# Expert stage with eight experts known beforehand, five of them loaded when it begins, and down weights issued by ScalarE

## The reference, cut to what matters

```python
N_GROUPS, EXP_PER_GROUP, TOP_K, D_EXPERT = 4, 8, 2, 256       # 32 experts
h2 = modulate(rmsnorm(x, g_ffn), sh_m, sc_m)
x = x + gt_m[:, None, :] * hier_moe(h2, ...)

def hier_moe(h, ...):
    g_logits = h @ w_rg + b_rg;  g_sel = argmax(g_logits)      # one group of eight
    e_logits = h @ w_re + b_re                                 # inside it, the best two experts
    top_v, top_i = lax.top_k(e_in, TOP_K)
    w2 = softmax(top_v) * p_g
    a = h @ w_gate[e];  b = h @ w_up[e]                        # 1024 x 256 each
    act = silu(a) * b * gate
    return act @ w_down[e]                                     # 256 x 1024
```

## Time and profile before

| | |
|---|---|
| timed runs | 1287.98, 1291.29, 1291.51 us; median 1291.29 |
| profiled execution, its own time | 1291.53 us |
| its span | 1289.9 us (19011 instructions) |
| PE busy | 1182.8 us (92%), ACT 356.3 (28%), DVE 672.3 (52%), POOL 212.8 (16%) |
| expert stage's first list read to the end | 968.8 to 1289.9 us |
| DMA over the span | 213.47 MB, mean 165 GB/s |
| weight loads of 1024 KB by SP in the expert stage | 84 |

### The profile page before, as it was taken

How to read it: one execution, slowest core, us unless ns; L and a number is a source line. 1 busy time by engine, 2 the same in 40 slices (tenths; PEclk the granted TensorE clock), 3 DMA queues, 4 the chain that set the end, 5 groups by cost and what they waited for, 6 DMA issues and landing times. The chain is left out here.

```text
span 1289.9 us, 19011 instructions
## 1 busy us (share of the span) xinstructions
PE 1182.8 (92%) x7174; PEld 662.3 (51%) x7175; DVE 672.3 (52%) x1313; ACT 356.3 (28%) x781; POOL 212.8 (16%) x250
## 2 busy tenths in 40 slices
PE   4999999999978997899999999899976999977995
PEld 1555555555543556666677776555543433332331
DVE  1255443554465884567777775544462554433443
ACT  1122222222222444265555553323320000000000
POOL 4000000000000002254443322011022212211111
PEclk9899999999998998889999999899977999988998
DMA  8721211111137871421111005362447999999993
GB/s 361 297 66 33 66 53 46 53 45 54 41 122 226 300 275 58 124 58 30 29 29 30 2 1 165 121 231 89 184 152 285 337 367 367 382 395 377 357 348 65
DMA packets 92834, 213.47 MB, mean 165 GB/s; under 512 B 20673, under 2 KB 54707, under 8 KB 77394
## 3 DMA queue, kind: packets, MB, share of 16 engines
q1 hardware_dynamic: 82258, 195.02, 41.1%
q0 software_dynamic: 7200, 17.33, 5.4%
q10 hardware_dynamic: 3296, 0.02, 0.1%
HBM read 185.03 MB, written 34.13 MB: 170 GB/s over the span
## 5 line engine op out<-in xcount | busy, mean ns | idle before, releaser
L2404 PE MATMUL g_GU<-w_gu,first_region 128*32 128x512 f32 (+2 forms) x656 | 143.0, 624 | 17.0 <-issue 17.0
L1921 PE MATMUL f_C<-first_region,oT 128*128 128x512 f32 x256 | 115.2, 603 | 0.0
L454 PE MATMUL U<-region,b_hT 128*128 128x512 f32 x256 | 112.3, 592 | 0.0
L2614 DVE TENSOR_TENSOR g_sig<-g_GU,g_sig 128x256 f32<-128x256 f32 x23 | 9.8, 425 | 165.8 <-ACT g_sig L2564 157.7
L1723 DVE TENSOR_TENSOR_SCAN region<-region,early 128x128 f32<-128x128 f32 (+7 forms) x64 | 88.6, 1404 | 6.3 <-POOL region L1530 6.3
L2404 PEld LDWEIGHTS g_GU<-w_gu,first_region 128*32 128x32 f32 (+2 forms) x656 | 43.2, 127 | 84.3 <-issue 83.4
L454 PE MATMUL b_UL<-region,b_hT 128*128 128x384 f32 (+1 forms) x256 | 76.5, 458 | 3.3 <-DMA region<-w_in 3.3
L1921 PEld LDWEIGHTS f_C<-first_region,oT 128*128 128x128 f32 x256 | 48.0, 193 | 54.3 <-issue 54.2
L454 PEld LDWEIGHTS U<-region,b_hT 128*128 128x128 f32 x256 | 47.5, 190 | 54.2 <-issue 54.0
L2383 POOL DMA_INDIRECT y<-oT,g_li x23 | 36.4, 1584 | 227.0 <-DVE oT L2632 133.8
L1592 PE MATMUL e_Z<-first_region,region 104*128 104x512 f32 (+3 forms) x192 | 70.8, 507 | 0.1
(11 more groups left out here) (489 smaller groups left out, 2160.2 us busy)
## 6 DMA issues: line engine op xcount, KB each, us to landing
w_gu<-w_gate SPq DMA_DIRECT2D x21, 1024.0 KB
w_gu<-w_up SPq DMA_DIRECT2D x21, 1024.0 KB
w_down<-w_down SPq DMA_DIRECT2D x21, 1024.0 KB
region<-w_ada SPq DMA_DIRECT2D x16, 1024.0 KB, 7.0
region<-w_in SPq DMA_DIRECT2D x3, 2048.0 KB, 17.5
oT<-w_gate SPq DMA_DIRECT2D x6, 1024.0 KB
oT<-w_up SPq DMA_DIRECT2D x6, 1024.0 KB
oT<-w_down SPq DMA_DIRECT2D x6, 1024.0 KB, 20.2
```

The costliest lines, as they stand in the source:

```text
L454: end = nc.tensor.matmul(dst[0:T, 0:c1 - c0], lhsT=hT[:, k, 0:T], rhs=g.w_in[:, k, c0:c1], start=k == 0, stop=k == KD - 1)
L1921: end = nc.tensor.matmul(C[n % 2][:, c * 512:(c + 1) * 512], lhsT=g.oT[:, i, k, :], rhs=wo[:, k, c * 512:(c + 1) * 512], start=k == 0, sto ...
L2404: end = nc.tensor.matmul(GU[h * n:h * n + n, :], lhsT=xT[:, b, k, h * n:h * n + n], rhs=wgu[s][:, :, k, :], start=k == 0, stop=k == KD - 1 ...
L2614: mark(nc.vector.tensor_tensor(sig[:], GU[:, 0:DE], sig[:], ALU.mult))
```

## The change

Eight experts are fixed in place of four: 0, 8, 16, 24, 4, 12, 20 and 28 in positions 0 to 7. Five of them are loaded in the norm stage in place of four. The fifth lies in a new region, slot_region, that holds the norm stage's modulation rows (f_rows in the old code) until the last tile is done. The fourth slot's loads are issued ahead of the last store of h2, right behind the last store of x2; the fifth slot's loads stand where the fourth's stood.

The fixed experts don't have a whole block each any more. They go four in three blocks (96 and 32 rows), so blocks 0 to 5 hold all eight. There are still 23 blocks: 18 of the form 96 and 32, three pairs and two whole ones (before: 12, five and six).

In the expert stage SP issues gate and up only, and waits for gu_mm only. The down weights are issued by ACT on its own queue, after the copy of the hidden values of block b for the experts whose slot was last used by block b-1. The lists of blocks 0 and 1 are read by two DMAs each.

The diff, cut to its core:

```diff
-FIXED = 4
+EVERY = 4
+FIXED, RESIDENT = NE // EVERY, 5
@@ phase_fr
-        rows = m.sb("f_rows", [P, 3, 2, D])
+        rows = g.slot_region[:].rearrange("p (a b n) -> p a b n", a=3, b=2)
@@ phase_fr, sync: the loop over tiles
+                if n == END:
+                    sp.wait_ge(pr_mm, NT)
+                    load_gate_up(nc, io, g, sp, early[3], 3, g.wgu_in[3])
+                    load_down(nc, io, g, sp, early[3], 3, g.wd_in[3])
                 sp.wait_ge(h2_done, n + 1)
                 sp.dma_start(g.h2_dram[i * P:i * P + T, :], h2[0:T]).then_inc(st_h2, 16)
                 if n in (1, 2, 6):
                     q = min(n - 1, 2)
-                    load_gate_up(nc, io, g, sp, q * EPG, q, g.wgu_in[q])
-                    load_down(nc, io, g, sp, q * EPG, q, g.wd_in[q])
-            sp.wait_ge(pr_mm, NT)
-            load_gate_up(nc, io, g, sp, 3 * EPG, 3, g.wgu_in[3])
-            load_down(nc, io, g, sp, 3 * EPG, 3, g.wd_in[3])
+                    load_gate_up(nc, io, g, sp, early[q], q, g.wgu_in[q])
+                    load_down(nc, io, g, sp, early[q], q, g.wd_in[q])
+            load_gate_up(nc, io, g, sp, early[4], 4, g.wgu_in[4])
+            load_down(nc, io, g, sp, early[4], 4, g.wd_in[4])
...
-                row = b * EPG * REGION
-                sp.dma_start(g.li[b][:], g.list_dram[row:row + P, :]).then_inc(g.li_in[b], 16)
+                list_parts(nc, g, sp, b, blocks[b], fixed_expert)
@@ phase_fr, vector: four more small steps at the start, one at the end
+            for half in range(EPG // EVERY):
+                sortable = groups(key[:])[:, :, half * EVERY + 1:(half + 1) * EVERY]
...
@@ expert_blocks
-    fixed = [whole(p) for p in range(FIXED)]
-    blocks = fixed[0:3] + paired[0:1] + fixed[3:4] + fours[0] + fours[1] + paired[1:2] + single[0:1] + paired[2:3]
-    return blocks + single[1:2] + paired[3:4] + fours[2] + fours[3] + paired[4:5]
+    fixed = [four_in_three([p, p + 1, p + 2], p + 3) for p in range(0, FIXED, NG)]
+    blocks = fixed[0] + fixed[1] + paired[0:1] + single + fours[0] + fours[1] + paired[1:2] + fours[2] + fours[3]
+    return blocks + paired[2:3]
@@ phase_g, sync: weights
                 load_gate_up(nc, io, g, sp, expert(p), s, wgu_in[s])
-                if instead[p] is not None:
-                    sp.wait_ge(dn_mm, instead[p] + 1)
-                load_down(nc, io, g, sp, expert(p), s, wd_in[s])
-            for p in order[FIXED:]:
+            for p in order[RESIDENT:]:
                 weights(p)
@@ phase_g, scalar
+            late = order[RESIDENT:]
+            def down_in(p):
+                load_down(nc, io, g, act, expert(p), place[p], wd_in[place[p]])
+            for p in late:
+                if instead[p] is None:
+                    down_in(p)
...
                 if b + AHEAD < NB:
                     list_in(b + AHEAD)
+                for p in late:
+                    if b and instead[p] == b - 1:
+                        act.wait_ge(dn_mm, b)
+                        down_in(p)
```

More of the change, by code:

```diff
@@ L1758, in phase_fr @@
         ORDER = [0, PT] + list(range(1, PT))
+        blocks = expert_blocks()
+        early = []
+        for parts in blocks:
+            early += [fixed_expert(p) for p, _, _, _ in parts if p < FIXED and fixed_expert(p) not in early]
         GW = 8
@@ L2129, in constants @@
                 step(V.tensor_copy(cum[0:1, 0, :], first_row[0:1, :]))
-                step(V.tensor_scalar(ei[:], pair[0:NE, 0, 0, 0:1].bitcast(I32), EPG - 1, None, ALU.bitwise_and))
+                step(V.tensor_scalar(ei[:], pair[0:NE, 0, 0, 0:1].bitcast(I32), EVERY, None, ALU.bitwise_and))
+                step(V.tensor_scalar(own[:], ei[:], 0.0, None, ALU.is_gt))
+                step(V.tensor_scalar(ei[:], pair[0:NE, 0, 0, 0:1].bitcast(I32), EVERY - 1, None, ALU.bitwise_and))
                 step(V.tensor_scalar(rank[:], ei[:], 0.0, None, ALU.is_equal))
@@ L2133, in constants @@
                 step(V.tensor_scalar(base[:], pair[0:NE, 0, 0, 0:1], 1.0 / EPG, -float(FIXED), ALU.mult, ALU.add))
+                step(V.scalar_tensor_tensor(base[:], own[:], NG - EVERY / EPG, base[:], ALU.mult, ALU.add))
                 step(V.tensor_scalar(base[:], base[:], rank[:], float(FIXED), ALU.mult, ALU.add))
@@ L2251, in _ @@
             step(V.scalar_tensor_tensor(key[:], count[:], float(NE), idx[:], ALU.mult, ALU.add))
-            sortable = groups(key[:])[:, :, 1:]
-            step(V.scalar_tensor_tensor(sortable, grank[:].unsqueeze(2).broadcast_to([P, NG, EPG - 1]), -SIDE / 2.0, sortable,
-                                        ALU.mult, ALU.add))
+            for half in range(EPG // EVERY):
+                sortable = groups(key[:])[:, :, half * EVERY + 1:(half + 1) * EVERY]
+                step(V.scalar_tensor_tensor(sortable, grank[:].unsqueeze(2).broadcast_to([P, NG, EVERY - 1]), -SIDE / 2.0,
+                                            sortable, ALU.mult, ALU.add))
             step(V.tensor_tensor(eq[0:NE], key[0:NE], g.ident[0:NE, 0:NE], ALU.mult))
@@ L2257, in _ @@
             others = eq[0:NE, 0:NE - FIXED]
-            step(V.tensor_scalar(others.rearrange("p (a e) -> p a e", a=NG), groups(key[0:NE])[:, :, 1:], own[:], None,
+            step(V.tensor_scalar(others.rearrange("p (a e) -> p a e", a=FIXED), lots(key[0:NE])[:, :, 1:], own[:], None,
                                  ALU.is_gt))
@@ L2284, in load_down, with fixed_expert, list_parts @@
     engine.dma_start(g.w_down[b][:], io["w_down"][e].rearrange("(p k) n -> p k n", p=P)).then_inc(sem, 16)
+def fixed_expert(p):
+    return p % NG * EPG + p // NG * EVERY
+def list_parts(nc, g, engine, b, parts, expert):
+    for p, row, n, at in parts:
+        engine.dma_start(g.li[b][at:at + n, :], g.list_dram[bass.ds(expert(p) * REGION + row, n), :]).then_inc(g.li_in[b], 16)
 def expert_blocks():
@@ L2332, in phase_g @@
         holding = {}
-        order = list(range(FIXED)) + [p for p in order if p >= FIXED]
         for q, p in enumerate(order):
@@ L2433, in _ @@
         def _(sp):
-            experts = {r: r * EPG for r in range(FIXED)}
+            experts = {p: fixed_expert(p) for p in range(FIXED)}
             def expert(r):
@@ L2789, in program @@
             g.w_down.append(part[:, 2 * KD * DE:2 * KD * DE + 2 * D].rearrange("p (k n) -> p k n", n=D))
+        g.slot_region = m.sb("slot_region", [P, 2 * KD * DE + 2 * D])
+        g.w_gu.append(g.slot_region[:, 0:2 * KD * DE].rearrange("p (w k n) -> p w k n", w=2, k=KD))
+        g.w_down.append(g.slot_region[:, 2 * KD * DE:].rearrange("p (k n) -> p k n", n=D))
         g.y = turned[:, 6 * KD * P:8 * KD * P].rearrange("p (b n) -> p b n", b=2)
@@ L2794, in program @@
         phase_fr(nc, io, g)
-        for b in range(FIXED, 6):
-            weight_slot(b)
+        weight_slot(5)
         phase_g(nc, io, g)
```

2 lines of the change are left out of this document (added).

## The result

| | us, median | span of the runs | ratio to before, 95% interval |
|---|---|---|---|
| before | 1291.4 | 1287.98 to 1291.95 (6 runs) | 1 |
| after | 1297.61 | 1296.29 to 1299.15 (6 runs) | 1.0053 [1.0043, 1.0063] |

The changed kernel is slower by some 6 us. That lies inside the predicted range (1282 to 1301), but 5 us above the predicted value, and beyond the 0.3% that I had called no change. "Slower" had a chance of 0.29 from me, "no change" 0.40. The profiled execution took 1296.73 us with a span of 1295.1; before, the span was 1289.9.

What follows compares the result with a forecast made beforehand. The expert stage was taken as bound by PE, with late weights costing 24.0 us. Terms: 1291.5 + 0 - 1.9 + 1.3 + 1.8 + 0.7 - 0.7 = 1292.7, against the median 1292.5; range 1282 to 1301 us.

Steps and rivals of the forecast that it cites:

- A fifth expert loaded ahead: Expert stage: three loads (7.7 us) leave it, but the lead is lost to full slots; taken as 0, bounds -3.1 to 0.
- The ledger's first stall: Expert stage: count of loads and per-block work put PE's first wait at block 12 or 13, 3 to 8 us.
- The later stalls: Expert stage from block 13 on: both kernels need the same experts at the same blocks, so these waits were left unchanged.
- SP doesn't wait for dn_mm: SP's queue in the expert stage: DMA idle time at 1190 us goes; -1.9 us, bounds -4.7 to 0.
- Down loads on ACT's queue: Expert stage: downs under way can hold up urgent gate and up loads; +1.3 us, bounds 0 to 10.2.
- End of the norm stage: SP's queue before the expert stage: more loads ahead of the list reads delay its start; +1.8 us, bounds +0.4 to +5.3.
- Blocks 1 and 2, and the gather of block 2: Early expert stage: longer blocks cost +0.7 us, a gather landing sooner gives -0.7; the two cancel.
- The second queue takes its turns: Rival, expert stage: each of four stalls grows by a whole down load, 10.2 us, giving 1301.6 us; chance 0.12.
- POOL's results out: Rival, expert stage: result transfers become the bound, deciding from about 12.1 us per landing; +11.9, 1305.2 us; chance 0.08.
- The lead holds: Rival, expert stage: the fifth expert's lead and all saved idle time reach PE, giving about 1283 us; chance 0.28.
- the DMA share from 980 to 990: Sign, early expert stage: this share of the DMA engines' time falls well under 0.9.
- the idle time of g_GU: Sign, PE in the expert stage: the prediction is wrong if this falls under 10 us or rises over 25.

Runs made afterwards that it cites:

- e3: Changed kernel with four experts loaded ahead in place of five, norm-stage loads at their old places: 1297.32 us, ratio 1.0067.
- e1: Changed kernel with the down loads back on SP's queue in the old order, behind its wait for dn_mm: 1291.35 us, ratio 1.0018.
- e2: Kernel before with only the down loads moved to ACT's queue: 1297.22 us, ratio 1.0060.
- e8: Changed kernel with ACT issuing each down one turn before its expert's first use, not when its slot is free: 1292.34 us, ratio 1.0013.
- e11: Kernel before with each down on SP's queue behind gate and up loads of experts that start no later: 1290.55 us, ratio 0.9997.
- e4: Changed kernel with all expert-stage loads on SP's queue in the order of need: 1291.85 us, ratio 1.0014.
- e6: Changed kernel with lists read into partitions in another order, spreading their empty places: 1301.95 us, ratio 1.0102.
- e5: Kernel before with lists read into partitions in another order, spreading their empty places: 1300.51 us, ratio 1.0076.

## Why the prediction was half right

- **A fifth expert loaded ahead: 0.** The stage is as long with four as with five (290.1 and 289.9 us from block 0 to 22), as the value says; e3's level median leaves a doubt of 3 us. On one queue the lead was gone early: by 1040 us e1 had moved 28.6 loads and the kernel before 29.4 (the bytes of SP's and ACT's queues from 971 us on, and three loads for each expert loaded ahead). Of this, 1.0 load is e1's later start, 2.6 us.
- **The ledger's first stall, at block 12 or 13, 3 to 8 us.** Wrong for the changed kernel, where none came until block 16; right for e1 (5.32 us at block 12). The later stalls, which I had let stand, went at block 15 and rose at 16 and 19, from 5.17 and 1.46 us to 10.87 and 10.71. The ledger counted every load in one line. With the downs on a queue of their own, block 12's gate and up loads had no waiting down ahead of them.
- **SP doesn't wait for dn_mm: -1.9 (-4.7 to 0).** Too small. The early share rose from e1's 0.81 to 0.95, worth up to 6.3 us by 1040. A part of that only makes good the idle time of e1's full slots: against the kernel before (0.93) the changed kernel was 1.9 loads ahead by 1040 (31.3 against 29.4), 4.9 us. I had looked for the gap of the earlier trace rows at 1190 and taken the early idle time for full slots alone.
- **Down loads on ACT's queue: +1.3 (0 to +10.2).** This is the step that failed, in its size. Together with the gain just named I had -0.6 us for the split; it cost 4.5 us net in the new order (after against e1, by the ratios) and 7.7 in the old one (e2 against before). I had argued that a down can only disturb a gate and up load while both are under way, and that ACT issues none while PE stands still. What counts is the whole stage: the downs that had run ahead by the time of a stall, 1.7 and 3.0 loads, each 2.56 us. With 1.33 downs per block (1.4 MB in 11.76 us) on a queue of its own, ACT's queue is seldom behind, while SP's is; that could have been worked out beforehand.
- **End of the norm stage: +1.8 (+0.4 to +5.3).** 3.2 in the profile, and 2.9 between e3's wait for the list and this one; inside the bounds.
- **Blocks 1 and 2, and the gather of block 2.** Right. X's wait of 0.73 us for that gather went, and 0.94 came for the hidden values in its place.
- **The rivals.** *The second queue takes its turns* named the mechanism nearly: late gate and up loads, at the price of whole downs. It had four stalls grow by one down each. They became two, 5.7 and 9.3 us longer than before, with 1.7 and 3.0 downs ahead of them. The Trainium skill (DMA: Bandwidth & Descriptors, Queues, rings and completion order) says that each DMA engine goes round robin between the queues that have work. The rows agree in part: q1 and q10 had 49.9% and 25.3% of the engines' time up to block 19, not equal halves, as q10 has only half as many bytes to bring. Here the queue with little to bring kept up (25.0 downs, all that could be issued), and the one that was late got the rest. *POOL's results out*: they landed after 12.6 us as I had worked out (12.7), which is over the 12.1 from which I had them decide, but PE waited for them 1.08 us. The stalls for weights hid the rest. e8, with results nearly as slow, has the time back. *The lead holds* was true from block 13 to 15, 11.5 us ahead, and false at the end.
- **The range.** It held the time partly by luck: an early gain that I had too small and an overtaking that I had much too small stand against each other. Of the signs, the DMA share from 980 to 990 fell as foretold (0.71, 1.00 before), and the idle time of g_GU stayed between 10 and 25 us (21.6), but no stall came at block 12 or 13.
- The Trainium skill (the same page, Issuing engines are not separate DMA queues) says that issuing from several engines saves only the sequencer's time. These runs disagree in both directions: 0.81 to 0.95 of DMA share early, as a wait on one queue no longer holds the other, and 4.5 us lost in all, because the order of service changed.

In the changed kernel the granted clock was 0.62 over the stall at block 16, which is the 1.2 GHz level for most of it, and 0.72 over the 9.70 us of products behind it (stretches as above):

```profile
1170.80:1181.70 10.90, 0.04 (x1) 0.02 (x1) 2.83 (x3) 0.39 (x1) 0.45 (x1) 0.62 1.02 374
1181.70:1191.40 9.70, 9.69 (x66) 2.69 (x66) 1.22 (x2) 0.00 (x0) 2.17 (x2) 0.72 0.96 348
1196.30:1203.30 7.00, 7.00 (x69) 2.19 (x72) 1.29 (x2) 0.39 (x1) 1.36 (x2) 1.00 1.03 394
```

The DMA share is 1.02 through the whole stall: the engines are full, with other weights than those PE needs. The slow products cost 2.7 and 2.2 us now, 4.9 in all, and 7.0 before. So the stage's 4.6 us are made up of +4.6 of stalls (21.6 less 17.0), -2.1 of slow products, +1.1 of the wait for POOL and +0.7 for blocks 1 and 2, which is +4.3.

What stays open are e3's 3 us, and why a load completes only when some three loads beyond it have been moved, on one queue as well.

No kernel beat the one before; e11 equals it.

## What to carry to other kernels

When a stage is bound by its transfers, a second queue is no extra bandwidth, but a change in who is served. The stream with work that is needed late must not be able to run ahead of the one that PE waits for, so either keep both on one queue in the order of need, or tie the issue of the late stream to the consumer's progress and not to free slots. Here either gave the loss back (e4, e8), and neither beat the old order on one queue. Count the bytes that have landed when a stall ends, compare them with those that were needed by then, and set the surplus beside that of one queue (here about three loads): what is over that is the price. A DMA share of 1 during the stall doesn't say that the right bytes are moving.

## What had not been expected of the hardware

- A read of a small list costs ACT about 0.95 us to issue in the kernel before, and 1.8 when its rows are described 8 apart: 19.79 us for 11 in place of 11.41 for 12. In the changed kernel it is 0.83 (9.90 for 12), and 1.2 in e6 (14.46 for 12). The sigmoid that stands behind them came 8.0 us later in e5 (995.13 instead of 987.10).
- A list scatter into HBM, followed by list reads, grew from 4.92 to 8.11 us between the last scatter's issue and the first gather with three more loads in front; a gather beside three fresh loads takes 8.63 us instead of about 4.3.
- The results out land after 10.4 us beside one stream of weights and 12.6 us beside two, both with a share of 1.02 to 1.03 between 1040 and 1130 us.
